# Hybrid decoder layer: penalty, scale and row maximum of the attention scores in one VectorE instruction per head

## What is computed

```python
slopes = 2.0 ** (-8.0 * (arange(8) + 1) / 8)
scale = HEAD_DIM ** -0.5                         # 1/8, on q
s = einsum('bqhc,bqkc->bqhk', ql, kv)
dist = (t[None, :, None] - idx)
s = s - slopes[None, None, :, None] * dist[:, :, None, :]
s = where((dist >= 0)[:, :, None, :], s, -inf)
p = softmax(s, axis=-1)
```

## Time and profile before

| | us |
|---|---|
| median of 3 runs | 1208.52 |
| lowest, highest run | 1207.38, 1208.82 |
| the profiled execution, its own time | 1206.98 |
| its span, first to last instruction | 1205.1 |
| PE busy | 1164.1 |
| DVE busy | 578.6 |
| ACT busy | 407.8 |
| POOL busy | 308.4 |

### The profile page before, as it was taken

One profiled execution on the slowest core, in us unless ns is written; L12 is line 12 of the kernel. 1 busy time (PEld: TensorE's weight loads), 2 busy tenths in 40 slices (PEclk: granted clock), 3 DMA queues, 4 the chain that ended last, 5 costly groups with the idle time before them and its releaser, 6 DMA issues.

```text
span 1205.1 us, 14862 instructions
## 1 busy us (share of the span) xinstructions
PE 1164.1 (97%) x5459; PEld 916.5 (76%) x5459; DVE 578.6 (48%) x831; ACT 407.8 (34%) x636; POOL 308.4 (26%) x238
## 2 busy tenths in 40 slices
PE   6899999998999999999999999999999999999997
PEld 2588888887888878667666667887888888888885
DVE  4644444444344252579987665646333333332331
ACT  3433333332122232133544555424232232322223
POOL 0399999999974010000000000000000000000000
PEclk9999999999999999999999999999999999999999
DMA  9675574565543224212121112221324233242221
GB/s 337 175 222 163 168 225 156 167 228 175 195 153 111 72 54 130 71 35 71 53 54 45 50 47 88 88 75 48 122 70 131 78 93 116 70 135 93 86 70 70
DMA packets 156857, 138.22 MB, mean 115 GB/s; under 512 B 3359, under 2 KB 151186, under 8 KB 156818
## 3 DMA queue, kind: packets, MB, share of 16 engines
q1 hardware_dynamic: 127668, 108.33, 28.9%
q10 hardware_dynamic: 29150, 29.37, 7.6%
HBM read 135.59 MB, written 2.10 MB: 114 GB/s over the span
## 4 chain that ended last, share of the span: by engine, by line
PE 61%; POOL 16%; issue 10%; DVE 8%; ACT 4%; POOLq 1%; ACTq 0%; DVEq 0%
PE ps L345 18%; PE ps L347 18%; PE ps L346 18%; POOL ada L1337 9%; POOL ada L1333 7%; DVE prob L1252 2%; DVE nmax L1255 2%; ACT prob L1035 1%; PE ps L906 1%; DVE score L1219 1%; ACT probT L1044 1%; PE ps L881 1%; DVE max L1217 1%; PE ps L891 1%; ACT w_hi L322 1%
## 5 line engine op out<-in xcount | busy, mean ns | idle before, releaser
L327 DVE TENSOR_TENSOR w_lo<-raw,w_hi 128x1024 fp32r<-128x1024 f32 (+1 forms) x168 | 243.7, 1451 | 438.1 <-ACT w_hi L322 438.1
L345 PE MATMUL ps<-h_hi,w_hi 128*128 128x512 f32 x1024 | 412.6, 403 | 6.1 <-DVE h_lo L433 3.2
L347 PE MATMUL ps<-h_hi,w_lo 128*128 128x512 f32 x1024 | 400.6, 391 | 0.0
L346 PE MATMUL ps<-h_lo,w_hi 128*128 128x512 f32 x1024 | 400.5, 391 | 0.0
L322 ACT ACTIVATE w_hi<-raw 128x1024 fp32r<-128x1024 f32 (+1 forms) x168 | 187.6, 1117 | 318.3 <-PE ps L347 317.7
L345 PEld LDWEIGHTS ps<-h_hi,w_hi 128*128 128x128 f32 x1024 | 193.3, 189 | 62.3 <-issue 15.1
L347 PEld LDWEIGHTS ps<-h_hi,w_lo 128*128 128x128 f32 x1024 | 192.9, 188 | 41.0
L346 PEld LDWEIGHTS ps<-h_lo,w_hi 128*128 128x128 f32 x1024 | 193.4, 189 | 36.4 <-issue 0.5
L1337 POOL TENSOR_TENSOR ada<-ada 128x512 f32<-128x512 f32 x112 | 142.5, 1273 | 8.8
L345 PE MATMUL ps<-g_hi,w_hi 128*128 128x512 f32 x352 | 140.1, 398 | 0.0
L346 PE MATMUL ps<-g_lo,w_hi 128*128 128x512 f32 x352 | 138.1, 392 | 0.0
(11 more groups left out here) (163 smaller groups left out, 885.4 us busy)
## 6 DMA issues: line engine op xcount, KB each, us to landing
raw<-in_w_ffn SPq DMA_DIRECT2D x42, 1024.0 KB, 5.4
ada<-in_w_ada ACTq DMA_DIRECT2D x28, 1024.0 KB, 6.5
raw<-in_w_ffn SPq DMA_DIRECT2D x16, 1408.0 KB, 6.2
raw<-in_w_in SPq DMA_DIRECT2D x64, 256.0 KB, 3.2
ada<-in_w_ada SPq DMA_DIRECT2D x8, 1024.0 KB, 14.3
raw<-in_w_out SPq DMA_DIRECT2D x16, 256.0 KB, 3.0
x_tok<-in_x SPq DMA_DIRECT2D x4, 512.0 KB, 5.3
raw<-in_w_ffn SPq DMA_DIRECT2D x4, 512.0 KB, 10.8
```

The costliest lines, as they stand in the source:

```text
L327: nc.vector.tensor_tensor(tiles_of(w_lo[j % SPL], nk), raw_of(f, j, nk), tiles_of(w_hi[j % SPL], nk).bitcast(F32), ALU.subtract).then_inc( ...
L345: nc.tensor.matmul(ps[:, bank, :], hi, rhs_hi, start=start, stop=False)
L346: nc.tensor.matmul(ps[:, bank, :], hi, rhs_lo, start=False, stop=False)
L347: return nc.tensor.matmul(ps[:, bank, :], lo, rhs_hi, start=False, stop=stop)
```

## The change

The two instructions of a head's penalty and the shared row maximum become one `tensor_tensor_reduce` per head. It reads the score from PSUM and the distances, adds them, multiplies by a constant, writes the product and gives the minimum of the row. The slope therefore moves: q is scaled by 1/(8 slope) when it is evacuated (a column `q_scale` with one value per partition, filled by eight small memsets at the start), so that score plus distance times minus slope is the negated final score; its minimum is the negated maximum. `exps` multiplies by -1.0 on the way in. The semaphore `s_used` is gone: `m_done` counts heads, the exponential of each head waits for its own head, and `scores(m)` waits for both heads of the step before.

```diff
+SLOPES = [2.0 ** (-8.0 * (h + 1) / HEADS) for h in range(HEADS)]
+FAR = 3.0e38
...
+        q_scale = at("q_scale", [HP], msc + 3776)
...
-                pe.wait_ge(s_used, 2 * m)
+                pe.wait_ge(m_done, 2 * m)
...
-                    copy_out(u, dst[:, hp, :], scale=HEAD_DIM ** -0.5 if q < 8 else 1.0)
+                    copy_out(u, dst[:, hp, :], scale=q_scale[:, hp:hp + 1] if q < 8 else 1.0)
...
-                act.wait_ge(m_done, m + 1)
                 for e in range(2):
+                    i = 2 * (m % 2) + e
                     p = prob[m % 2][:, e, 0:(c + 1) * P]
-                    nc.scalar.activation(p, p, ACT.Exp, bias=nmax[:, 2 * (m % 2) + e, :],
-                                         accum_out=psumq[:, 2 * (m % 2) + e, :]).then_inc(e_done, 1)
+                    act.wait_ge(m_done, 2 * m + e + 1)
+                    nc.scalar.activation(p, p, ACT.Exp, bias=nmax[:, i, :], scale=-1.0,
+                                         accum_out=psumq[:, i, :]).then_inc(e_done, 1)
...
+            for hp in range(HP):
+                for e in range(2):
+                    nc.vector.memset(q_scale[64 * e:64 * e + 64, hp:hp + 1], HEAD_DIM ** -0.5 / SLOPES[2 * hp + e])
...
-                    nc.vector.tensor_scalar(dst[n], ps[:, 4 + n % 3, :], HEAD_DIM ** -0.5, None, ALU.mult).then_inc(prj_free, 1)
+                    nc.vector.tensor_scalar(dst[n], ps[:, 4 + n % 3, :], q_scale[:, n - 2:n - 1], None, ALU.mult).then_inc(prj_free, 1)
...
                 for e in range(2):
-                    slope = 2.0 ** (-8.0 * (2 * hp + e + 1) / HEADS)
                     dve.wait_ge(s_psum, 2 * m + e + 1)
-                    nc.vector.scalar_tensor_tensor(prob[m % 2][:, e, 0:w], d, slope, ps[:, B_S[e], 0:w],
-                                                   ALU.mult, ALU.add).then_inc(s_used, 1)
-                dve.wait_ge(s_used, 2 * m + 2)
-                nc.vector.tensor_reduce(nmax[:, 2 * (m % 2):2 * (m % 2) + 2, 0], prob[m % 2][:, :, 0:w], AX.X, ALU.max,
-                                        negate=True).then_inc(m_done, 1)
+                    nc.vector.tensor_tensor_reduce(prob[m % 2][:, e, 0:w], ps[:, B_S[e], 0:w], d, -SLOPES[2 * hp + e], FAR,
+                                                   ALU.add, ALU.min, nmax[:, 2 * (m % 2) + e, :]).then_inc(m_done, 1)
```

More of the change, by code:

```diff
@@ L226, in build_layer @@
         s_psum = sem("s_psum")
-        s_used = sem("s_used")
         m_done = sem("m_done")
```

## The result

| | kernel before | changed kernel |
|---|---|---|
| median of the runs | 1207.95 us (4 runs, 1206.60 to 1208.82) | 1199.12 us (4 runs, 1197.38 to 1199.33) |
| profiled execution, span | 1206.98, 1205.1 | 1199.33, 1197.6 |
| ratio | | 0.992, 95% interval 0.9901 to 0.9939 |

The changed kernel is faster by 0.8%. The forecast was 1200.0, in a range of 1198.5 to 1204.5; the median is 0.9 us under the forecast, and the fastest run, 1197.38, lies under the range. The gain forecast was 8.5 us. The two medians differ by 8.8 us and the two profiled executions by 7.65; by the ratio the gain is 1208.52 x 0.008 = 9.7 us, with 7.4 and 12.0 as ends. Taken from the kernel before's median of 1207.95, the ratio puts the changed kernel at 1198.3 us, 0.2 us under the range.

The account below looks back on a forecast made before the run. PE was taken as the bound, idle 8.69 us in the attention stage through late exponentials. Long delays of 6.9 us plus 1.6 in small pieces gave 8.5, so 1208.52 - 8.5 = 1200.0 us, range 1198.5 to 1204.5.

Parts of the forecast that it names:

- PE's idle time in the attention stage is what counts, and all but 0.80 us of it goes: PE idles 8.69 us in the attention stage; 8.5 us are gained and the 0.80 before the last values stays.
- The cause is that the exponentials are late: DVE-ACT loop: copies wait for late exponentials; the change starts the copies after steps 22 and 23 3.1 us earlier.
- the work theory: Main rival in the experiments: the gain comes from DVE having less work; no chance was given.
- Pace of the new instruction, 1.05 ns per element: On DVE, the fused instruction runs at the old penalty's pace, 0.68 us for w = 512.
- the half-pace rival: Fused instruction on DVE takes about 2.1 ns per element; gain only 4 us, 1204.5 us; chance 0.11.
- The small read, 0.10 us: DVE's small instruction writing each head's minimum costs 0.10 us, with 0.08 and 0.17 as ends.
- the later release of the banks: `scores(m)` waits for `m_done`, 0.2 us later than `s_used` after `biased` starts; only the first steps lose 0.2 us.
- What each head's own wait brings: Exponentials on ACT, costed by heads: step 22 (w = 384) saves 1.36 us, step 23 (w = 512) 1.72.
- The sign turns at f near 0.75: If a head costs f us above the old penalty, DVE fills its period; slower beyond 0.75; fixed-price rival, chance 0.07.
- my later recount: Expectation for 0.69 us more per head: attention stage 2 to 5 us over the kernel before, 1210 to 1213 us.
- From the stage's 8.5 us to the time and its range: Whole kernel: 8.5 us off the median 1208.52 gives 1200.0; 8-in-10 range 1198.5 to 1204.5.
- The low end, 1198.5: Lower end of the range for the whole kernel: 0.2 us more PE idle gained, and runs differing by 1.4 us.

Follow-up runs that it names:

- run 3: Kernel before with the maximum taken per head behind its penalty, not fused, each exponential waiting for its own head: 1205.31 us, ratio 0.9968.
- run 5: Changed kernel with two extra additions of 256 elements on DVE behind each normalisation, off the path: 1198.84 us, ratio 0.9932 to the kernel before.
- run 2: Changed kernel, but each exponential waits for both heads as before the change: 1199.46 us, ratio 0.9934 to the kernel before.
- run 6: Changed kernel with one extra 256-element addition ahead of each fused instruction, 0.41 us more per head: 1199.95 us, ratio 0.9940 to the kernel before.
- run 7: Changed kernel with extra additions of 256 and 128 elements ahead of each fused instruction, 0.69 us more per head: 1208.82 us, ratio 1.0005.
- run 1: The changed kernel measured again, nothing altered: 1199.39 us, ratio 0.9918 to the kernel before.
- 9: Changed kernel with three merge matmuls issued ahead of the last values, filling PE's last idle: 1198.77 us, ratio 0.9923 to the kernel before.
- run 12: The kernel before, unchanged, profiled again for another trace: 1202.23 us in one run.
- run 8: Changed kernel with two extra 256-element additions ahead of each fused instruction, 0.82 us more per head: 1217.25 us, ratio 1.0081 to the kernel before.

## Where the prediction held, and the step that failed

- *PE's idle time in the attention stage is what counts, and all but 0.80 us of it goes.* Shown. The changed kernel's only wait of PE in the stage is the one of 0.80; the stage is 8.6 us shorter (8.5 summed), and all behind it keeps its 474.6 us.
- *The cause is that the exponentials are late.* Shown by runs 3 and 5, against the work theory. By the rule of the Trainium skill that was weighed ("VectorE: DVE Perf Modes", rules for kernel authors: minimize the count of operations) nothing would be gained: four instructions instead of three; run 3 has four as well and gains too. What counts in this stage is the way from the scores to the last exponential, not the count.
- *Pace of the new instruction, 1.05 ns per element.* Right: 0.68 us for 512. So the half-pace rival falls. The Trainium skill's rule on two non-bf16 SBUF sources ("Vector Engine (DVE) Microarchitecture Reference", section 7) does not bear on this form, which has one of its sources in PSUM.
- *The small read, 0.10 us.* Mis-sized: its row has 0.08 us, but DVE's pace with it is the same as without, 0.61 us from head to head. So w = 512 saves 1.83 us instead of 1.72, and the later release of the banks, put at 0.2 us, is nearly nothing (one wait, of 0.5 us at PE's weight load). DVE's busy time fell by 26.5 instead of 20 us for the same reason: what was removed came off whole.
- *What each head's own wait brings.* The prediction costed the two exponentials by heads; run 2 shows that this part could be left out. Delays of 1.6 to 2.2 us had to be outrun: the 2.2 us that run 2 saves were just enough, and the changed kernel saves 3.3 (1.44 and 1.83; 3.1 were summed). I didn't ask how much slack would be left, and so costed run 6 too high: with 0.41 us more per head 1.7 us are lost where I had 4.5.
- *The sign turns at f near 0.75.* f counts what a head costs above the old penalty. With the read at nothing, run 7 has f = 0.69 and stands at 1.0005 (0.9985 to 1.0026), its stage 1.8 us longer than before. The figure was right within 0.1, in part by luck: some 1.3 us of run 7's stage are a fall of the clock, which was in no sum. Of my later recount (1210 to 1213, stage 2 to 5 us longer) the low end met the stage and missed the time, 1208.82.
- *From the stage's 8.5 us to the time and its range.* This is the step that failed. The low end, 1198.5, is the forecast less 1.5 us, and was argued from two terms: 0.2 us more of PE's idle time, and "the runs differ by 1.4 us", read off three runs. The first held, the second was far too small. In 59 later runs the kernel before took 1201.39 to 1211.20, a spread of 9.8 us, and the changed kernel 1193.69 to 1200.14 in the six of run 1. And the gain was put at what the stage's idles last in one trace, with nothing for what the clock does behind an idle. The measured gain is 9.7 us by the ratio (7.4 to 12.0), 8.8 between the medians beside it and 9.3 between those of run 1, 1208.70 and 1199.39, against 8.6 in the stage of the traces.

Whether the 0.2 to 1.1 us beyond the stage are more than noise isn't shown: 8.6 lies within the interval. If they are real, their cause stays open, with one candidate. Of the 59 runs of the kernel before, 22 had a mean clock of 0.988 or 0.989 and took 1208.25 to 1211.20, while no run of the changed kernel and its close kin (25 runs: 1, 2, 5, 9) was under 0.990. None of the three traces of the kernel before has a fall of the clock in the attention stage, but run 3's has one, behind an idle of 1.68 us at the same scores where the kernel before idles 1.50, and it cost 1.3 us. If each of the 22 runs had one such fall more, that would be 1.3 x 22/59 = 0.5 us in the mean, by an estimate from these figures. The change removes these idles, so it would remove that cost too.

## What to carry to other kernels

Where one engine is busy nearly all the time, list its waits with what each waits for, and follow one of them back around the loop; the price of the change is how much later or earlier that chain ends, capped by the wait. A relief of another engine's load is worth nothing by itself (run 5 gave it all back for 0.8 us), and a saving in the chain beyond the wait is worth nothing either (run 2). Check the slack before polishing, and take the spread of the runs from many of them when you set a range.

## What the runs showed of the hardware

**The granted clock behind an idle.** In run 12, the kernel before, and in run 2, which is close to the changed one, the attention stage begins some 5 us earlier than in the other traces of each. In most traces PE waits 3.6 us for POOL's column sums near 300 us; in run 2's it waits 1.28, in run 12's not at all. The windows of run 1 around this place (granted clock in the third column from the end):

```profile
290.00:302.00 12.00, 8.36 (x39) 7.04 (x38) 5.55 (x4) 3.85 (x4) 11.37 (x9) 0.93 0.63 205
302.00:310.00 8.00, 8.00 (x26) 6.31 (x26) 2.55 (x3) 0.02 (x1) 7.53 (x7) 0.68 0.40 133
```

and the same of run 2's trace:

```profile
290.00:302.00 12.00, 10.60 (x49) 8.73 (x49) 6.95 (x6) 4.35 (x5) 11.00 (x9) 1.00 0.67 215
302.00:310.00 8.00, 8.00 (x38) 6.63 (x37) 2.80 (x4) 1.39 (x1) 7.61 (x6) 1.00 0.35 122
```

Behind an idle of 3.65 us the clock was 0.68 in the next 8 us, part of them at 1.2 instead of 2.4 GHz, and PE started 26 matmuls instead of 38; behind 1.28 us it stayed at 1.00. In run 8 the idle of 3.12 us at 652.8 was followed by 0.66 over 650 to 660. Short idles can go either way: the ones of 1.5 to 2.1 us in the attention stage of the kernel before left the clock at 1.00 in all three of its traces, while the one of 1.68 us in run 3 was followed by 0.50 over 648 to 650. The Trainium skill ("TensorE: Matmul & The Clock Gate", Part 1: The HAM clock gate) says that a PE array which has been idle runs at half its clock until it has been busy again; the 0.68 behind 3.65 us and the 0.50 behind 1.68 us agree, and the 1.00 behind idles of up to 2.1 us shows that not every idle has this price. Why POOL is late in most runs and not in all wasn't looked into.

**The read of the accumulator costs nothing here.** The small instruction behind the fused one has a row of 0.08 us and starts in the same moment as the next head's instruction (675.07), which starts 0.61 us after the first. Two old penalties follow each other as closely: both take 1.28 us from 680.84 on, one of them 0.68, so the second starts 0.60 us behind the first.
